# Every second choice of slots 12 to 44 summed on DVE in SBUF instead of on PE

## What is computed

```python
def _peer_tokens(h, w_q, keys, u_tab, v_tab):
    q = (h @ w_q).reshape(T, PEER_HEADS, 2, PEER_DKH)
    s = jnp.einsum('tpsd,psnd->tpsn', q, keys).astype(jnp.float32)
    s1, i1 = lax.top_k(s[:, :, 0], PEER_TOPK)
    s2, i2 = lax.top_k(s[:, :, 1], PEER_TOPK)
    ...
    sc, sel = lax.top_k(cand, PEER_TOPK)
    eidx = jnp.take_along_axis(cidx, sel, axis=-1)
    gate = jax.nn.softmax(sc, axis=-1)
    u = u_tab[eidx]
    act = jax.nn.gelu(jnp.einsum('td,tpkd->tpk', h, u).astype(jnp.float32))
    return jnp.einsum('tpk,tpkd->td', (gate * act).astype(h.dtype), v_tab[eidx])
```

## Time and profile before

| | |
|---|---|
| Time, median of 3 runs | 3788.89 us (3787.71 to 3788.89) |
| Time of the profiled execution | 3789.96 us |
| Its span | 3788.2 us |
| Busy in the span: PE, DVE, ACT, POOL | 3195.6, 2033.8, 1372.4, 1224.8 us |
| First gather issued, last matmul of a slot begun | 818.4 us, 3779.1 us |
| Gathers | 1152, 1208.03 MB |

### The profile page before, as it was taken

How to read it: one execution, slowest core, us unless ns; L and a number is a source line. 1 busy time by engine, 2 the same in 40 slices (tenths; PEclk the granted TensorE clock), 3 DMA queues, 4 the chain that set the end, 5 groups by cost and what they waited for, 6 DMA issues and landing times.

```text
span 3788.2 us, 33212 instructions
## 1 busy us (share of the span) xinstructions
PE 3195.6 (84%) x9934; PEld 1529.3 (40%) x9934; DVE 2033.8 (54%) x4955; ACT 1372.4 (36%) x4012; POOL 1224.8 (32%) x1184
## 2 busy tenths in 40 slices
PE   7999998559878977977897897788789779877777
PEld 4565555446224422622442362244235225422222
DVE  2333333166655665665566566556656655764444
ACT  2232321023434344343434434343443434343333
POOL 0000001014434334433444443334444344443332
PEclk9999998589999999999999999999999999999999
DMA  5010011439999999999999999999999999999998
GB/s 213 20 38 19 21 36 39 144 145 408 415 421 414 410 418 408 404 422 420 401 405 422 408 408 422 422 408 405 420 411 402 417 421 416 412 422 416 421 422 350
DMA packets 198596, 1272.94 MB, mean 336 GB/s; under 512 B 29329, under 2 KB 33041, under 8 KB 50705
## 3 DMA queue, kind: packets, MB, share of 16 engines
q0 software_dynamic: 165888, 1208.03, 77.5%
q1 hardware_dynamic: 20960, 37.86, 2.9%
q10 hardware_dynamic: 11584, 25.17, 1.8%
HBM read 1260.10 MB, written 11.80 MB: 336 GB/s over the span
## 4 chain that ended last, share of the span: by engine, by line
DMA 39%; PE 27%; issue 6%; ACT 6%; DVE 2%; ACTq 1%; POOL 0%; DVEq 0%; POOLq 0%
DMA e_uv<-uv,e_expert 39%; PE psum L1021 21%; PE psum L1006 6%; ACT e_diag L1089 2%; ACT e_weight L1084 1%; ACT e_gl L1082 1%; ACT L1082 1%; PE psum L987 1%; DVE e_product L1235 1%; POOL e_uv L935 0%; ACTq L1099 0%; ACT L1071 0%; DVE e_chosen L1211 0%; ACT L1095 0%; ACT e_squares L1094 0%
## 5 line engine op out<-in xcount | busy, mean ns | idle before, releaser
L1021 PE MATMUL psum<-e_uv,e_diag 128*128 128x512 f32 x4608 | 2255.4, 616 | 511.0 <-ACT e_diag L1089 510.3
L1235 DVE SCALAR_TENSOR_TENSOR e_product<-e_uv,e_h 128x1024 f32<-128x1024 f32 x1152 | 1411.1, 1225 | 1192.9 <-DMA e_uv<-uv,e_expert 1178.9
L935 POOL DMA_INDIRECT e_uv<-uv,e_expert x1152 | 1192.0, 1035 | 1846.6 <-PE psum L1021 1701.7
L1021 PEld LDWEIGHTS psum<-e_uv,e_diag 128*128 128x128 f32 x4608 | 798.5, 191 | 1773.9 <-ACT e_diag L1089 1164.1
L1082 ACT ACTIVATE e_gl<-e_dots 128x1 f32<-128x1 f32 x1152 | 233.1, 202 | 1572.6 <-DVE e_product L1235 1571.1
L1089 ACT ACTIVATE e_diag<-e_ident,e_weight 128x128 f32<-128x128 f32 x1152 | 462.2, 401 | 37.7
L436 PE MATMUL psum<-w_in_sb,hT_sb 128*128 128x512 f32 (+1 forms) x864 | 344.4, 560 | 15.7 <-DMA w_in_sb<-w_in 15.7
L1084 ACT ACTIVATE e_weight<-e_gl,e_gate 128x1 f32<-128x1 f32 x1152 | 339.1, 294 | 37.4
L1006 PEld LDWEIGHTS psum<-e_hT,e_w_q 128*128 128x128 f32 x2304 | 299.8, 193 | 124.0 <-issue 122.4
L1006 PE MATMUL psum<-e_hT,e_w_q 128*128 128x128 f32 x2304 | 301.2, 276 | 1.1 <-ACT e_hT L1047 1.1
L436 PEld LDWEIGHTS psum<-w_in_sb,hT_sb 128*128 128x128 f32 x864 | 164.4, 191 | 188.7 <-issue 185.0
(11 more groups left out here) (164 smaller groups left out, 1513.7 us busy)
## 6 DMA issues: line engine op xcount, KB each, us to landing
e_uv<-uv,e_expert POOLq DMA_INDIRECT x1152, 10.3
w_in_sb<-w_in ACTq DMA_DIRECT2D x5, 2048.0 KB, 19.6
e_w_q<-w_q ACTq DMA_DIRECT2D x4, 2048.0 KB, 20.1
xT_sb<-xT SPq DMA_DIRECT2D x9, 512.0 KB, 4.5
xt_sb<-x SPq DMA_DIRECT2D x9, 512.0 KB, 3.6
x<-xt_sb SPq DMA_DIRECT2D x9, 512.0 KB, 2.6
e_xt<-x SPq DMA_DIRECT2D x9, 512.0 KB, 11.7
e_y<-x SPq DMA_DIRECT2D x9, 512.0 KB, 8.3
```

Of the source, the lines that this page charges most:

```text
L935: eng.indirect_dma_start(out=uv[n % RING][:, :], out_offset=None, in_=dr["uv"], in_offset=bass.IndirectOffsetOnAxis(ap=expert[:, t % 2, k: ...
L1021: mm = eng.matmul(psum[:, b * BANK:(b + 1) * BANK], diag[n % DIAGS][:, :], uv[n % RING][:, D + half * BANK:D + (half + 1) * BANK], start=( ...
L1235: eng.scalar_tensor_tensor(out=product[n % 2][:, :], in0=uv[n % RING][:, 0:D], scalar=1.0, in1=h[:, t % 2, :], op0=ALU.mult, op1=ALU.mult, ...
```

## The change

The diff marks 17 slots of each of the first eight tiles (even `k` from 12 to 44) and slot 12 of the last one as DVE's: 137 of 1152. A slot so marked has no `diag` and no matmul. DVE adds weight times `v` to a new buffer `y2` in SBUF instead, two slots later (`LAG`), straight after the dot product of slot `k + 2`. The first such sum of a tile reads `y`, so the residual enters there; `add_residual` then adds PSUM to `y2`. POOL waits for the engine that sums slot `n - 6`. The dot product's unread output now goes over the `u` half in place of `product`.

```diff
+def on_dve(n):
+    j, k = divmod(n, CHOSEN)
+    return 12 <= k < 46 and k % 2 == 0 if j < TILES - 1 else k == 12
...
+    LAG = 2
...
-        product = [sb(f"product{i}", [P, D]) for i in range(2)]
+        y2 = sb("y2", [P, D])
...
                     if n >= RING:
-                        eng.wait_ge(added, n - RING + 1)
+                        m = n - RING
+                        if on_dve(m):
+                            eng.wait_ge(dve_added, dve_adds(m + 1))
+                        else:
+                            eng.wait_ge(pe_added, pe_adds(m + 1))
...
             def add_expert(t, k):
                 n = t * CHOSEN + k
+                if on_dve(n):
+                    return
+                d = pe_adds(n)
...
+                if on_dve(n):
+                    return
+                d = pe_adds(n)
                 eng.wait_ge(weight_ready, n + 1)
-                if n >= DIAGS:
-                    eng.wait_ge(added, n - DIAGS + 1)
...
                 eng.wait_ge(uv_loaded[n % RING], 16 * (n // RING + 1))
-                if n >= 2:
-                    eng.wait_ge(dot_ready, n - 1)
                 if k == 0:
                     eng.wait_ge(h_ready, t + 1)
-                eng.scalar_tensor_tensor(out=product[n % 2][:, :], in0=uv[n % RING][:, 0:D], scalar=1.0,
+                eng.scalar_tensor_tensor(out=uv[n % RING][:, 0:D], in0=uv[n % RING][:, 0:D], scalar=1.0,
                                          in1=h[:, t % 2, :], op0=ALU.mult, op1=ALU.mult,
                                          accum_out=dots[:, t % 2, k:k + 1]).then_inc(dot_ready, 1)
 
+            def add_choice(t, k):
+                n = t * CHOSEN + k
+                d = dve_adds(n)
+                first = d == dve_adds(t * CHOSEN)
+                eng.wait_ge(weight_ready, n + 1)
+                if first:
+                    eng.wait_ge(x1_loaded, 16 * (t + 1))
+                else:
+                    eng.wait_ge(dve_added, d)
+                eng.scalar_tensor_tensor(out=y2[:, :], in0=uv[n % RING][:, D:2 * D], scalar=weight[:, t % 2, k:k + 1],
+                                         in1=(y if first else y2)[:, :], op0=ALU.mult, op1=ALU.add)\
+                   .then_inc(dve_added, 1)
+
             def add_residual(t):
-                eng.wait_ge(added, CHOSEN * (t + 1))
-                eng.wait_ge(x1_loaded, 16 * (t + 1))
-                eng.tensor_tensor(y[:, :], y[:, :], psum[:, t % 2 * 2 * BANK:(t % 2 * 2 + 2) * BANK], ALU.add)\
+                eng.wait_ge(pe_added, pe_adds(CHOSEN * (t + 1)))
+                eng.wait_ge(dve_added, dve_adds(CHOSEN * (t + 1)))
+                eng.tensor_tensor(y[:, :], y2[:, :], psum[:, t % 2 * 2 * BANK:(t % 2 * 2 + 2) * BANK], ALU.add)\
                    .then_inc(sum_ready, 1)
...
                     dot_expert(t, k)
+                    if k >= LAG and on_dve(t * CHOSEN + k - LAG):
+                        add_choice(t, k - LAG)
                     if t and k == SUM_AT:
                         add_residual(t - 1)
```

More of the change, by code:

```diff
@@ L813, in after, with dve_adds, pe_adds @@
         self.wait()
+def on_dve(n):
+    j, k = divmod(n, CHOSEN)
+    return 12 <= k < 46 and k % 2 == 0 if j < TILES - 1 else k == 12
+DVE_BEFORE = [0]
+for _n in range(TILES * CHOSEN):
+    DVE_BEFORE.append(DVE_BEFORE[-1] + on_dve(_n))
+def dve_adds(n):
+    return DVE_BEFORE[n]
+def pe_adds(n):
+    return n - DVE_BEFORE[n]
 def stage_experts(nc, psum, dr):
+    LAG = 2
     RING = 6
@@ L907, in stage_experts @@
         diag_ready = sem("diag_ready")
-        added = sem("added")
+        pe_added = sem("pe_added")
+        dve_added = sem("dve_added")
         x1_loaded = sem("x1_loaded")
@@ L1015, in add_expert @@
                 n = t * CHOSEN + k
+                if on_dve(n):
+                    return
+                d = pe_adds(n)
                 if k == 0 and t >= 2:
                     eng.wait_ge(sum_ready, t - 1)
-                eng.wait_ge(diag_ready, n + 1)
+                eng.wait_ge(diag_ready, d + 1)
                 for half in range(2):
                     b = t % 2 * 2 + half
-                    mm = eng.matmul(psum[:, b * BANK:(b + 1) * BANK], diag[n % DIAGS][:, :],
+                    mm = eng.matmul(psum[:, b * BANK:(b + 1) * BANK], diag[d % DIAGS][:, :],
                                     uv[n % RING][:, D + half * BANK:D + (half + 1) * BANK],
                                     start=(k == 0), stop=(k == CHOSEN - 1))
-                mm.then_inc(added, 1)
+                mm.then_inc(pe_added, 1)
             eng.wait_ge(made, 3)
@@ L1085, in weigh_expert @@
                    .then_inc(weight_ready, 1)
+                if on_dve(n):
+                    return
+                d = pe_adds(n)
                 eng.wait_ge(weight_ready, n + 1)
-                if n >= DIAGS:
-                    eng.wait_ge(added, n - DIAGS + 1)
-                eng.activation(diag[n % DIAGS][:, :], ident[:, :], ACT.Copy, scale=weight[:, at[0], at[1]])\
+                if d >= DIAGS:
+                    eng.wait_ge(pe_added, d - DIAGS + 1)
+                eng.activation(diag[d % DIAGS][:, :], ident[:, :], ACT.Copy, scale=weight[:, at[0], at[1]])\
                    .then_inc(diag_ready, 1)
@@ L1219, in route @@
                 if t >= 2:
-                    eng.wait_ge(added, CHOSEN * (t - 1))
+                    eng.wait_ge(pe_added, pe_adds(CHOSEN * (t - 1)))
+                    eng.wait_ge(dve_added, dve_adds(CHOSEN * (t - 1)))
                 eng.scalar_tensor_tensor(out=expert[:, t % 2, :], in0=chosen[:, 0, :], scalar=float(NKEYS),
```

## The result

The changed kernel takes 3851.6 us (median of 4 runs, 3849.39 to 3863.61) against 3788.89 (3787.71 to 3790.92, 4 runs): ratio 1.0171, 95% interval 1.0150 to 1.0193, slower by 63 us in the medians. 3830 us was forecast, in a range of 3788 to 3870. The profiled execution took 3863.61 us (span 3861.9), the longest of the four, so its stretches add up to 73.7 us of span and not to 63.

The account below looks back on a forecast made before the run. Gathers and PE were taken to set the pace by turns, PE lagging beside the query products. Lag removed -26.8, residual wait +25.1 and searches +43 made +41 us on the profiled 3789.96, a median of 3830 us; range 3788 to 3870.

Parts of the forecast that it names:

- PE's lag: Slots 38 to 48, tiles 0 to 7: PE falls behind beside the query products; removing this wins 26.8 us.
- What was costed at nothing: Dropped dot wait, dot's new output place and `add_residual` reading `y2`: no cost, since the dot waits for its later gather.
- The first sum's wait: Slot 12's sum, behind slot 14's dot, waits for the residual's load and holds gather 18: 25.1 us lost.
- That just fits, with nothing to spare: Even slots without a search: dot to landing four slots on takes 9.98 us, due after 9.94.
- The searches: Top-16 searches in slots with sums make DVE late, so gathers land late: 5.3 us a tile, 43 in eight.
- The sum: Whole kernel: -26.8 + 25.1 + 43 = +41 us, a median of 3830 us.
- the ring stays short throughout: Rival, slots 14 to 48: nothing refills the ring, each DMA hiccup shows; +74 us, 3863; 22 in 100.
- Absorbed, and faster: Rival: gathers need less time from POOL's start, 5.9 us deciding, so delays are absorbed; 3775 us; 15 in 100.
- Even, with POOL not held up: Rival: POOL's instruction takes 0.94 us for 1.8 and landing 4.9 for 5.4; 3788 us; 9 in 100.
- PE's clock: Rival: PE with thinned slots is granted half its clock; 3995 us or so; 2 in 100.

Follow-up runs that it names:

- the best kernel: Changed kernel with two residual buffers, LAG 1 and DVE sums only in slots 16, 18, 20, 22, 24, 31, 33, 39, 41: 3766.49 us, ratio 0.9932.
- a bare stop: DVE wait for the residual's load behind slot 14's dot, tiles 1 to 7, added to the 3766.49 us kernel with few sums at LAG 1: 3771.81 us.
- the filler: Two short one-input maxima on DVE behind each sum without a search piece, added to the changed kernel with two residual buffers: 3809.56 us against 3831.76.

## Why the prediction was right, and where not

**PE's lag (-26.8 us): right.** Slots 38 to 48 take 222.57 us in the best kernel, 22.9 less than before, and 0.0068 of the time, 26 us, is what that kernel wins in all. No kernel here won more.

**What was costed at nothing: right** for the dots' output place and the dropped wait, which were tried alone; the sum's length, 1.28 us, came out at 1281 ns.

**The first sum's wait (25.1 us): right in size, in part by luck.** The profile shows 25.4 (21.2 and tile 8's 4.2); taking the wait out gave 24. It is dear because gather 18 hangs on the sum behind the stop, and started 1.66 us after the load's landing in each of the eight tiles; a bare stop with PE free to catch up cost 5. But the terms differ. The windows from the load's issue to slot 18's dot product, tiles 1 to 8 of the kernel after, add up to:

```profile
sum 128.83, DVE 39.43; mean DVE 4.93
```

That is 16.1 us each where 17.05 was the least foreseen, since gather 18 took 1.68 us in POOL and landed 4.5 to 4.8 us later (1.8 and 5.4 foreseen), and 16.0 more than before. About 10 us more lie before the load's issue, which was put at nothing: from slot 12's dot product to it these tiles took 50.7 us against 40.7, 6.3 of that in tile 5, which was to lose nothing.

**"That just fits, with nothing to spare": this step failed.** The loop from an even slot's dot product to that of four slots on was put at 9.98 us, against 9.94 allowed. In the mean of the same 112 loops the kernel after took 11.33: 2.70 to POOL's start (2.78 foreseen), 1.38 in POOL (1.8 foreseen), 7.05 to the landing (5.4 foreseen) and 0.21 until DVE took it. The landing is the term that was mis-sized, by 1.65 us. The 5.4 came from four late gathers of one tile; in the kernel before the even gathers of slots 38 to 48 took 6.1 from POOL's end in the mean over eight tiles, and that would have put the loop at 10.7 us, over the 9.94. Most of such a time is the wait behind the gather before: that one landed 2.9 us after POOL's end in the four of rows 9, 3.4 in slots 38 to 48 and 3.98 here, where the odd gather goes out right behind the even one; the even one landed 2.5, 2.8 and 3.07 us behind it. So 1.1 of the 1.65 us is the longer wait. Why the step between the two landings grew to 3.07 was not tried.

**The searches (43 us): wrong as a cause.** Even slots lose 1.34 us per loop before the searches (24 loops that end in slots 22 to 26: 11.28 us) and 1.40 in them (72 loops that end in slots 32 to 48: 11.34). A search does not make matters worse, since DVE, late or not, waits for a gather that is later: landing to dot is 0.29 us there (0.02 before the searches), and the shorter time in POOL's instruction, 1.25 us for 1.52, makes that good. At 1.39 us a loop, 62 loops cost 86 us, and the profile has 79.6 over pace, where 43 were forecast.

**The sum.** -26.8 + 25.1 + 43 was +41. With the measured terms it is -30.6 + 79.6 + 25.4, or +74, as the profiled execution has it (3863.61 less 3789.96); its runs' median is 12 us lower. The range held because the upper bound of the searches' term, 76 us, was taken from all 31 slots at the pace of a short ring. So the rival "the ring stays short throughout", 3863 us, told the profile's course better than the forecast did, though for another reason than hiccups: every even gather is issued too late by a loop that is too long. That the time lies inside the range is to that extent luck.

**The other rivals.** *Absorbed, and faster* needed a landing 5.9 us from POOL's start; it took 8.4 (1.38 and 7.05). With it falls what the prediction worked out from the Trainium skill (DMA: Bandwidth & Descriptors, Anatomy of one DMA), an estimate of 4.4 us, by which the change would have won. *Even, with POOL not held up*: in the kernel with two residual buffers the filler removed the hold and won 22 us, and it was still slower than before. *PE's clock*: see below.

## What to carry to other kernels

When buffers come from a ring, add up the whole loop, from the use of one buffer to the use of its next filling, term by term, and hold it against ring size times pace; work moved to an idle engine lengthens the loop by however much later it frees the buffer, whatever the engine's busy share. Take a landing time from many transfers in the state that the change will bring about, not from a few short ones: most of it can be the wait behind the transfer before. The same sums are a gain of 0.6% one slot earlier and with the first operand loaded a tile ahead.

## What the runs showed of the hardware

POOL's gather instruction takes 0.94 us alone and 1.81 when DVE starts a dot product (two inputs from SBUF) just ahead of it; two maxima with one input in that place leave it at 0.94 (89 gathers, 0.93 to 0.95 each), although in 82 of these the next dot product starts before POOL's instruction has ended. That is worth 22 us here. The Trainium skill (SBUF — State Buffer, Who interferes with whom) says that a VectorE instruction with two SBUF inputs contends with a GpSimd instruction that reads SBUF; the trace agrees so far as these operations go, while what part of the gather's instruction waits was not tried.

TensorE's granted clock fell where PE got gaps: 0.949 in the mean over the kernel after against 0.973 before. Windows of tile 2 in the kernel after, slots 18-26, 27-37 and 38-48:

```profile
1545.70:1572.39 26.69, 21.74 (x122) 16.14 (x120) 17.10 (x24) 7.14 (x24) 10.90 (x9) 0.97 0.97 369
1572.39:1604.02 31.63, 21.89 (x109) 14.89 (x110) 27.06 (x88) 9.52 (x31) 15.25 (x12) 0.95 0.98 378
1604.02:1633.87 29.85, 21.47 (x90) 13.16 (x89) 25.85 (x78) 8.64 (x30) 12.16 (x11) 0.89 0.98 375
```

Each mean lies between the levels of 1.2 and 2.4 GHz, nearer the upper. PE is busy 65 of 88 us there, and the gathers that wait for it, the odd ones, mostly followed the even ones with 0.30 us and no wait for PE (105 of 112, as above), so this fall sets hardly anything there; no run here had the full clock throughout.
